# A hybrid layer's forgetting attention, moved from half and eighth parts of the TensorE array to the whole of it

## The reference

```
proj = rmsnorm(x) @ w_in      # 512 u_pool, 512 z_pool, 512 q, 512 k, 512 v, 512 z_attn, 8 f, 1024 + 1024 gates
log_f = log_sigmoid(f_logit + b_forget)                 # (272 tokens, 8 heads)
c = cumsum(log_f)                                        # over the tokens
s[t, j] = q_t . k_j / sqrt(64) + c_t - c_j               # 8 heads of 64; causal; blocks of 128 queries
o = softmax(s) @ v
y_attn = o * silu(z_attn)
y_pool = causal_multiscale_pool(u_pool) * silu(z_pool)
merged = sigmoid(g_pool) * (y_pool @ w_up_pool) + sigmoid(g_attn) * (y_attn @ w_up_attn)
x = rmsnorm(x + merged @ w_out)[16:]
```

## Time and profile before

| | |
|---|---|
| timed runs | 1357.02, 1357.83, 1358.37 us |
| span of the profiled execution, first to last instruction | 1354.2 us |
| PE busy | 1299.4 us, 96% |
| DVE busy | 883.3 us, 65% |
| ACT busy | 712.4 us, 53% |
| POOL busy | 71.8 us, 5% |
| mean DMA rate | 153 GB/s |
| mean granted TensorE clock | 0.975 of full |

### The profile page before, as it was taken

How to read it: one execution, slowest core, us unless ns; L and a number is a source line. 1 busy time by engine, 2 the same in 40 slices (tenths; PEclk the granted TensorE clock), 3 DMA queues, 4 the chain that set the end, 5 groups by cost and what they waited for, 6 DMA issues and landing times.

```text
span 1354.2 us, 26405 instructions
## 1 busy us (share of the span) xinstructions
PE 1299.4 (96%) x10226; PEld 1248.9 (92%) x10226; DVE 883.3 (65%) x1500; ACT 712.4 (53%) x1033; POOL 71.8 (5%) x67
## 2 busy tenths in 40 slices
PE   7999999999999998898999999799999999999997
PEld 6878999999999997798999999699999968999996
DVE  7445778866655986635766665766665676766744
ACT  6434555665544765153665544565644444756532
POOL 6123000000000000250000000000000000000000
PEclk9999999999999999698999999899999998999999
DMA  8413454555654442000555652445564312555630
GB/s 324 147 72 127 163 186 158 212 184 182 220 194 141 168 154 104 1 2 8 181 186 185 222 212 93 156 157 186 190 251 148 125 66 77 177 185 184 247 125 31
DMA packets 48069, 207.53 MB, mean 153 GB/s; under 512 B 3200, under 2 KB 5376, under 8 KB 43648
## 3 DMA queue, kind: packets, MB, share of 16 engines
q1 hardware_dynamic: 46992, 203.89, 43.1%
q10 hardware_dynamic: 1008, 2.70, 0.6%
HBM read 205.53 MB, written 1.05 MB: 153 GB/s over the span
## 4 chain that ended last, share of the span: by engine, by line
PE 90%; DVE 6%; ACT 2%; issue 1%; DMA 0%; POOL 0%; ACTq 0%; DVEq 0%
PE main L1505 27%; PE main L1507 27%; PE main L1506 26%; PE main L1850 2%; PE side L1596 2%; PE side L1571 1%; DVE w_lo L792 1%; PE side L1553 1%; PE side L1554 1%; PE side L1891 1%; PE main L1835 0%; PE main L1905 0%; PE side L1559 0%; DMA x<-in_x 0%; ACT w_hi L428 0%
## 5 line engine op out<-in xcount | busy, mean ns | idle before, releaser
L1505 PE MATMUL main<-xg_hi,w_hi 128*128 128x256 f32 (+1 forms) x2024 | 573.0, 283 | 2.5 <-DVE w_lo L792 0.9
L1506 PE MATMUL main<-xg_hi,w_lo 128*128 128x256 f32 (+1 forms) x2024 | 571.5, 282 | 0.0
L1507 PE MATMUL main<-xg_lo,w_hi 128*128 128x256 f32 (+1 forms) x2024 | 571.2, 282 | 0.0
L428 ACT ACTIVATE w_hi<-raw 128x1024 fp32r<-128x1024 f32 (+2 forms) x364 | 404.5, 1113 | 307.9 <-PE main L1507 305.9
L792 DVE TENSOR_TENSOR w_lo<-raw,w_hi 128x1024 fp32r<-128x1024 f32 (+2 forms) x364 | 464.6, 1283 | 6.2 <-ACT w_hi L428 5.5
L1505 PEld LDWEIGHTS main<-xg_hi,w_hi 128*128 128x128 f32 x2024 | 384.0, 190 | 8.9 <-issue 4.7
L1507 PEld LDWEIGHTS main<-xg_lo,w_hi 128*128 128x128 f32 x2024 | 384.6, 190 | 0.0
L1506 PEld LDWEIGHTS main<-xg_hi,w_lo 128*128 128x128 f32 x2024 | 381.7, 189 | 0.2
L1507 PE MATMUL main<-h_lo,w_hi 128*128 128x256 f32 x704 | 199.2, 283 | 0.0
L1505 PE MATMUL main<-h_hi,w_hi 128*128 128x256 f32 x704 | 198.9, 283 | 0.0
L1506 PE MATMUL main<-h_hi,w_lo 128*128 128x256 f32 x704 | 197.3, 280 | 0.0
(11 more groups left out here) (352 smaller groups left out, 1513.8 us busy)
## 6 DMA issues: line engine op xcount, KB each, us to landing
raw<-in_w_gu_a SPq DMA_DIRECT2D x44, 1024.0 KB, 5.3
raw<-in_w_gu_b SPq DMA_DIRECT2D x44, 1024.0 KB, 5.3
raw<-in_w_down_a SPq DMA_DIRECT2D x16, 1408.0 KB, 6.0
raw<-in_w_down_b SPq DMA_DIRECT2D x16, 1408.0 KB, 6.1
raw<-in_w_in SPq DMA_DIRECT2D x20, 1024.0 KB, 5.3
raw<-in_w_in_a SPq DMA_DIRECT2D x13, 1024.0 KB, 5.2
raw<-in_w_up SPq DMA_DIRECT2D x4, 1024.0 KB, 5.3
raw<-in_w_out SPq DMA_DIRECT2D x4, 1024.0 KB, 5.2
```

What stands on the lines that cost most here:

```text
L428: act.activation(w_hi[:, u % RING, 0:n], raw[:, s % RAW, u % 2, 0:n], ACT.Copy).then_inc(hi_ready, 1)
L1505: pe.matmul(dst, a_hi, b_hi, start=first, stop=False)
L1506: pe.matmul(dst, a_lo, b_hi, start=False, stop=False)
L1507: return pe.matmul(dst, a_hi, b_lo, start=False, stop=last)
```

## The change

- q is kept per head with zeros in the other head's 64 rows (`qz`, cleared once by GpSimd), so the scores of a head are one matmul pair on 128 rows.
- The forget term no longer goes through TensorE. ScalarE's queue writes the 8 x 272 table `c8` to DRAM (slot 5) and reads it back to all 128 partitions (`cb`, slot 8); GpSimd adds mask and row per head into `bias` (two buffers), and VectorE's row maxima read `bias` in place of the constant mask.
- v is kept as 192 columns for each pair of heads, values, zeros, values, so that head a takes 128 columns with its own 64 in its own half. Both heads of a pair add into one region of 128 partitions; all eight stay in two PSUM banks (`side[2]`, `side[3]`), and the copies out (`take_output`) are gone: `y1` is formed from PSUM.
- The 16 meta keys are left out of each head. The probabilities of all eight heads stay in `s1` (8 buffers); at the end GpSimd gathers the 8 x 16 meta columns (`s_meta`), TensorE turns them at once (slot 22), and four matmuls with a block-diagonal `v_meta` (slot 23) add them to all heads. `v_meta` is made from the 16 x 512 meta values by a trip through DRAM (slots 12 and 15) and a product on GpSimd.
- The order of GpSimd's work, of the pool copies (one slot later) and the placement of buffers in SBUF follow from this.

The diff, without the placement of buffers, declarations and the index functions that follow from the new counts:

```diff
@@ scores, on TensorE
-                        r, h = slice(64 * (a % 2), 64 * (a % 2) + 64), a
-                        pe.matmul(dst, q1[r, h // 2, q], k1[r, h // 2, 0:n], start=True, stop=False)
-                        ins = pe.matmul(dst, ident[0:8, h:h + 1].to_broadcast([8, P]), c8[:, 0:n],
-                                        start=False, stop=True)
+                        ins = pe.matmul(dst, qz[:, a, q], k1[:, a // 2, 0:n], start=True, stop=True)
@@ new on TensorE, in place of outputs(a - 2) for these heads
+            def forget_outputs(a):
+                pe.wait_ge(pt_copied, a + 1)
+                pair, bank = a // 2, side[2 + a // 4]
+                at_c = pair % 2 * SEQ
+                for n, (_, _, first, _, _, col) in enumerate(key_blocks(a)):
+                    ins = pe.matmul(bank[:, at_c + first * P:at_c + SEQ],
+                                    v1[:, n, pair, 64 * (a % 2):64 * (a % 2) + P],
+                                    pt1[:, col:col + (2 - first) * P],
+                                    start=a % 4 == 0 and n == 0, stop=False, skip_group_check=True)
+                ins.then_inc(heads_done, 1)
+            def turn_meta():
+                pe.wait_ge(pt_copied, 8)
+                pe.wait_ge(s_meta_ready, 1)
+                for t in range(2):
+                    ins = pe.transpose(side[1][:, t * P:(t + 1) * P], s_meta[:, t, :], ident)
+                ins.then_inc(pt_ready, 1)
+            def meta_outputs():
+                pe.wait_ge(pt_copied, 9)
+                pe.wait_ge(v_meta_ready, 1)
+                for pair in range(4):
+                    ins = pe.matmul(side[2 + pair // 2][:, pair % 2 * SEQ:(pair % 2 + 1) * SEQ],
+                                    v_meta[:, pair * P:(pair + 1) * P], pt1[:, 384:640],
+                                    start=False, stop=True, skip_group_check=True)
+                ins.then_inc(meta_done, 1)
@@ TensorE's loop
-                    pe.wait_ge(c_ready, 1)
+                    pe.wait_ge(col_copied, 1)
...
+                if a == 10:
+                    turn_meta()
+                if a == 11:
+                    meta_outputs()
@@ row_maxima, on VectorE
+                if kind(a) == "forget":
+                    dve.wait_ge(bias_ready, a + 1)
+                    for t, (c, n) in enumerate(parts):
+                        ins = dve.tensor_tensor_reduce(
+                            out=buf[:, c:c + n], in0=score_bank(a)[:, c:c + n], in1=bias[:, a % 2, c:c + n],
+                            scale=1.0, scalar=-3e38, op0=ALU.add, op1=ALU.max,
+                            accum_out=row_max[:, i + t:i + t + 1])
+                    link(ins)
@@ VectorE's loop
-                if 0 < a - 3 < MEM_A and (a - 3) % 2 == 1:
-                    take_output(o1[:, (a - 3) // 2, :], a - 3)
...
-                    for j in range(3):
-                        n = META if j == 0 else P
-                        dve.tensor_scalar(v1[0:n, j, :], main[(t0 + 8 + j) % 4][0:n, :], rc1[0:n, j:j + 1], None,
-                                          ALU.mult).then_inc(evac, 1)
+                    dve.tensor_scalar(v_meta[0:META, :], main[(t0 + 8) % 4][0:META, :], rc1[0:META, 0:1], None,
+                                      ALU.mult).then_inc(evac, 1)
+                    dve.wait_ge(v_cleared, 1)
+                    for j in range(2):
+                        bank = main[(t0 + 9 + j) % 4][:, :].rearrange("p (g n) -> p g n", g=4)
+                        for c, at_c in ((0, 0), (64, 128)):
+                            ins = dve.tensor_scalar(v1[:, j, :, at_c:at_c + 64], bank[:, :, c:c + 64],
+                                                    rc1[:, j + 1:j + 2], None, ALU.mult)
+                        ins.then_inc(evac, 1)
+                if u < 4:
+                    unit_done(u)
+                    if u == 0:
+                        dve.wait_ge(q_cleared, 1)
+                    for i, rows in enumerate((slice(0, 64), slice(64, P))):
+                        ins = dve.tensor_tensor(qz[rows, 2 * u + i, :], main[(t0 + u) % 4][rows, 0:SEQ],
+                                                rstd[rows, META:TOK], ALU.mult)
+                    ins.then_inc(evac, 1)
...
-                    dve.wait_ge(o_copied, 4)
-                    dve.tensor_tensor(y1[:, :, :], o1[:, :, :], z_attn[:, :, :], ALU.mult).then_inc(y_done, 1)
+                    dve.wait_ge(meta_done, 1)
+                    for i in range(2):
+                        ins = dve.tensor_tensor(y1[:, 2 * i:2 * i + 2, :],
+                                                side[2 + i][:, :].rearrange("p (g n) -> p g n", g=2),
+                                                z_attn[:, 2 * i:2 * i + 2, :], ALU.mult)
+                    ins.then_inc(y_done, 1)
@@ copy_pt and loop, on ScalarE
-                if kind(a) == "forget":
-                    act.activation(pt1[0:META, 384:640], side[3][0:META, 0:256], ACT.Copy)\
-                       .then_inc(pt_copied, 1)
+                if u == 5:
+                    act.wait_ge(c_ready, 1)
+                    act.dma_start(c_row.rearrange("o (h n) -> (o h) n", h=8), c8[:, :]).then_inc(c_out, 16)
+                if u == 8:
+                    act.wait_ge(c_out, 16)
+                    act.dma_start(cb[:, :, :], c_row.rearrange("o n -> (o n)").partition_broadcast(P)
+                                  .rearrange("p (h n) -> p h n", h=8)).then_inc(c_in, 16)
+                if u == 12:
+                    act.wait_ge(evac, t0 + 9)
+                    act.dma_start(v_rows, v_meta[0:META, :]).then_inc(v_out, 16)
+                if u == 15:
+                    act.wait_ge(v_out, 16)
+                    act.dma_start(v_turn[:, :], v_rows.rearrange("j (h n) -> h j n", h=8)).then_inc(v_in, 16)
                 if u == 22:
+                    act.wait_ge(pt_ready, 9)
+                    act.activation(pt1[:, 384:640], side[1][:, 0:256], ACT.Copy).then_inc(pt_copied, 1)
+                    act.wait_ge(scores_ready, 8)
+                    act.dma_start(mem_x[:, :, :], dram["mem"]).then_inc(mem_in, 16)
@@ GpSimd
+            gp.memset(qz[:, :, :], 0.0).then_inc(q_cleared, 1)
+            gp.memset(v1[:, :, :, 64:P], 0.0).then_inc(v_cleared, 1)
...
+            def add_bias(a):
+                if a >= 2:
+                    gp.wait_ge(rowmax_ready, a - 1)
+                for t, (c, n) in enumerate(((0, 144), (144, 272))):
+                    ins = gp.tensor_tensor(bias[:, a % 2, c:c + n], const[:, K_MASK1 + c:K_MASK1 + c + n],
+                                           cb[:, a, 0:n], ALU.add)
+                ins.then_inc(bias_ready, 1)
```

More of the change, by code:

```diff
@@ L123, in copies_before @@
 def copies_before(a):
-    return 2 * min(a, MEM_A) + max(a - MEM_A, 0)
+    return a if a < MEM_A else a + 1
 def outputs_before(a):
-    return min(a, MLA) // 2 + max(a - MLA, 0)
+    return (min(a, MLA) - MEM_A) // 2 + max(a - MLA, 0)
 def program(nc, dram, out):
@@ L467, in copy_pt @@
             def copy_pt(a):
-                act.wait_ge(pt_ready, a + 1)
+                act.wait_ge(pt_ready, a + 1 if kind(a) == "forget" else a + 2)
                 if a > 0:
@@ L842, in row_maxima @@
                 else:
-                    if a >= 2:
-                        dve.wait_ge(pt_ready, a - 1)
-                    mask = K_MASK1 if kind(a) == "forget" else K_MASK2
+                    dve.wait_ge(pt_ready, a)
+                    mask = K_MASK2
                     for t, (c, n) in enumerate(parts):
@@ L1465, in _, with pool @@
                 gp.tensor_scalar(dst[:, :], dst[:, :], -PI_DOWN, None, ALU.max).then_inc(ang_ready, 1)
-            for g in range(4):
+            def pool(g):
                 gp.wait_ge(evac, FIRST_TILE["in1"] + 15 + g + 1)
@@ L1480, in _ @@
                   .then_inc(pooled_ready, 1)
-            gp.wait_ge(mask_in, 16)
+            def add_bias(a):
[5 more added lines that the diff above has]
+                ins.then_inc(bias_ready, 1)
+            gp.wait_ge(mask_in, 16)
+            gp.wait_ge(c_in, 16)
+            for a in range(6):
+                add_bias(a)
+            gp.wait_ge(v_in, 16)
+            gp.tensor_tensor(v_meta[:, :].rearrange("p (h n) -> p h n", h=8),
+                             v_turn[:, :].unsqueeze(1).to_broadcast([P, 8, 64]),
+                             const[:, K_BLK:K_BLK + 8].unsqueeze(2).to_broadcast([P, 8, 64]),
+                             ALU.mult).then_inc(v_meta_ready, 1)
+            pool(0)
+            add_bias(6)
+            pool(1)
+            add_bias(7)
+            pool(2)
+            pool(3)
+            gp.wait_ge(probs_ready, 16)
+            for t in range(2):
+                ins = gp.tensor_copy(s_meta[:, t, :].rearrange("p (h n) -> p h n", h=8),
+                                     s1[:, :, 144 * t:144 * t + META])
+            ins.then_inc(s_meta_ready, 1)
             gp.wait_ge(evac, FIRST_TILE["kt"])
@@ L1578, in outputs @@
                 which = kind(a)
```

(8 more changed lines are left out.)

94 lines of the change are left out of this document (57 added, 37 removed).

## The result

The changed kernel takes 1334.1 us (median of 4 runs, 1332.5 to 1336.0) against 1357.4: ratio 0.983 [0.982, 0.985]. Five later runs of it gave 1332.0 (1329.1 to 1337.4), ratio 0.982 [0.980, 0.984]. Over all nine its median is 1333.0; that of before, over all its runs on record, is 1357.3. So the change is worth 24.3 us, and the forecast of 1338.5 was about 5 us too high.

The account below looks back on a forecast made before the run. TensorE, busy 96% of the span, was taken as the bound. Matmuls -20.3, clock -1.4, head 0 +0.9, `s_meta` +1.0 and VectorE held up +0.5 make -19.3 us: from 1357.8 to 1338.5 us, range 1334.5 to 1345.

Parts of the forecast that it names:

- What bounds it: Whole kernel: TensorE bounds it, busy 96% of the span and 90% of the chain that ended last.
- Matmuls, -20.3: Attention matmuls on TensorE: 15.7 us in place of 36.0, at 1.7 ns a column on the whole array.
- Rival 2: Attention matmuls: whole-array ones cost the narrow price, 2.6 ns a column, saving less; 1348 us, chance 0.08.
- Clock, -1.4: Attention stretch: with no narrow matmul left, the fall to 1.2 GHz at 92.4 us does not come, saving 1.4 us.
- Head 0, +0.9: Behind unit 12: TensorE waits 0.9 us for VectorE's row maxima of head 0 to free the scores' bank.
- `s_meta`, +1.0: Slot 22: TensorE waits 1.0 us, between 0 and 6, for `s_meta` at the end of GpSimd's list.
- VectorE held up, +0.5: Attention slots: GpSimd's bias sums hold up VectorE's `w_lo` in a slot or two, 0.5 us (0 to 3).
- Rival 1: Slots 18 to 23: GpSimd becomes the bound, late biases also delaying VectorE; 1342 to 1347, say 1344 us, chance 0.19.
- Everything behind slot 24 only moves earlier: Behind the attention: a plain shift to earlier times, with the same units waiting for the same things.
- The sign that I had named for it: Behind the attention: times differing by more than the shift would show the forecast wrong on everything else.
- the two waits that were priced at 1.5 us: Attention slots: TensorE's wait for `s_meta`, 1.0 us, and VectorE held up by GpSimd's bias sums, 0.5 us.

Follow-up runs that it names:

- term_on_pe: The changed kernel with the forget term alone back on TensorE as 8-row matmuls, without the bias trip through DRAM and the bias sums: 1345.5 us.
- old_scores_outputs64: The changed kernel with scores on 64 rows, the 8-row forget term on TensorE and outputs at 64 weight columns again: 1347.8 us.
- bias_slot10: The changed kernel with the read-back of the bias asked for behind unit 10 in place of unit 8: 1335.0 us.
- gpsimd_plus6: The changed kernel with GpSimd's product `v_meta` made seven times over in place of once: 1340.0 us.
- before_plus32: The kernel before with every buffer behind the fixed ones 32 bytes further up in SBUF: 1355.1 us, ratio 0.998.
- after_again: The changed kernel run again without any edit: 1332.0 us.

## Why the prediction was right and where it failed

- **What bounds it:** right. TensorE is still busy 96% and makes 90% of the chain; nearly all that it lost came off the time.
- **Matmuls, -20.3:** right in sum. From 56.34 to 107.83 us are 51.5 us. Less 0.9 idle, 29.0 for units 12 to 21 and 5.7 for two more, 15.9 are left for the attention, where 15.7 was forecast. A head is 1.7. Rival 2 (narrow prices stay) is refuted, but its thought had a point: the price lies in shapes next to each other. With the 8-row term and narrow outputs present, scores on 128 rows would save next to nothing over 64 (13.6 less 10.5 for the term and 2.7 for the outputs leaves 0.4).
- **Clock, -1.4:** the fall in the stretch is gone, in both traces of the changed kernel. What took it away is open: before and its variants always had one or two there, yet term_on_pe and old_scores_outputs64 with their narrow matmuls had none, and bias_slot10 and gpsimd_plus6 got one behind a wait.
- **Head 0, +0.9:** 0.8, at the place and by the engine forecast.
- **`s_meta`, +1.0, and VectorE held up, +0.5:** both mis-sized, each measured 0. GpSimd was ready at 100.2 us, not 102 to 103: the list was counted right, but `v_turn` was back at 76.6 (78 forecast) and fewer operations met a `w_lo`. VectorE was held up, by 0.8 us in three of the heads and by less in others, and had the room. Rival 1 did not come; gpsimd_plus6 shows that it would have entered by bias 6, as the prediction named it.
- **Not forecast:** unit 12 began 0.5 us earlier (56.34 for 56.81). TensorE's first matmul begins as much earlier, at 8.29 for 8.78 us (8.34 for 8.90 in the runs made again), and its one wait from there to unit 12 is 0.4 us in both. What made the start earlier is open. The two rows:

```profile
8.78 0.60 PE L1505 MATMUL main<-xg_hi,wf_hi 128*128 128x272 f32 x1 [8.78 <-DMA const<-in_const]
```
```profile
8.29 0.60 PE L1591 MATMUL main<-xg_hi,wf_hi 128*128 128x272 f32 x1 [8.29 <-DVE xg_lo L857]
```

So the stretch gave -20.1 - 1.4 + 0.9 - 0.5 = -21.1 in place of -19.3.
- **The step that failed:** "Everything behind slot 24 only moves earlier: the same units wait for the same things." The waits are the same, but not the speed of 2112 matmuls, because `free0` moved by 32 bytes: -2.9, shown by before_plus32. The output projections and the `y` matmuls moved too: 120.0 and 120.3 ns a matmul before, 118.7 and 119.1 in after_again, -0.5 and -0.2 (in the first profile the first of the projections stayed at 120.0 ns). The sign that I had named for it, times behind that differ by more than the shift, is what gave it away.

Together -24.0, or -24.7 with the projections and `y`, against 24.3 by the medians and 19.3 forecast. The range failed because its lower end held only missing waits and the clock's luck, and no cause outside the stretch. Neither miss would have been enough alone: without the loops behind the stretch, or with the two waits that were priced at 1.5 us, the time would have come out inside the range.

## What to carry to other kernels

Where TensorE is the bound, count the steps between matmul shapes as well as the columns: a group on 64 rows or into 64 partitions between whole-array ones costs about 0.1 us on each side of a step (0.3 to 0.4 us a group here), which is more than the zeros of the padding cost. Work moved to an idle engine is free as long as its latest piece has slack; measure that slack at each buffer that is handed over, not only at the last. And after any edit to the layout compare the spacing of matmuls in untouched loops: where an operand lies can weigh as much as the edit.

## What the runs showed of the hardware

- The spacing of otherwise equal matmuls (128 rows, 128 columns, 256 moving, fp32r) goes from 113.3 to 120.0 ns with the place of the moving operand in SBUF; six places, the nearest 32 bytes apart, were tried. What in the chip makes it so is open.
- A VectorE `TENSOR_SCALAR` from SBUF to SBUF can be held up by GpSimd's sums, 0.57 to 1.36 us a pair.
- A wait of TensorE of 2.6 us was followed by 3.4 us at 1.2 GHz, one of 4.6 us went with 6.8; waits of 0.8 with none. But falls of 3.4 us also came without a wait.
